# Order changes around seven waits in a two-layer attention, RG-LRU and conv-FFN kernel

## The reference

```python
for l in range(DEPTH):                                   # DEPTH = 2
    mod = (silu(c) @ ada_w[l] + ada_b[l])                # six rows of 1024: shift, scale, gate, twice
    h = rms_norm(x, mix_pre_g[l]) * (1.0 + scale_m) + shift_m
    q, k, v, x_lru, gate = split(h @ w_in[l])            # 512, 128, 128, 512, 512 columns
    attn = sliding_window_attention(rope(q), rope(k), v, sinks[l])
    lru = rg_lru(causal_dwconv(x_lru, 4 taps)) * gelu(gate)
    y = concat([rms_norm(attn, g_attn[l]), rms_norm(lru, g_lru[l])]) @ w_out[l]
    x = x + gate_m * rms_norm(y, mix_post_g[l])
    h = rms_norm(x, ffn_pre_g[l]) * (1.0 + scale_f) + shift_f
    g, val = split(causal_dwconv(h @ ffn_w_up[l], 3 taps))   # 2 x 3072 columns
    y = (gelu(g) * val) @ ffn_w_down[l]
    x = x + gate_f * rms_norm(y, ffn_post_g[l])
```

## Time and profile before

| what | value |
|---|---|
| median of 3 runs | 1156.53 us (1156.14 to 1157.63) |
| profiled execution, its own time | 1151.1 us |
| its span, first to last instruction | 1149.3 us |
| PE busy | 1115.9 us, 97% |
| DVE busy | 803.3 us, 70% |
| ACT busy | 569.6 us, 50% |
| mean granted TensorE clock | 0.991 |

### The profile page before, as it was taken

The page is one execution under the profiler, slowest core; times in us unless marked ns, Lnnn a source line. Parts: engine busy times, 40 slices in busy tenths (PEclk is TensorE's granted clock), DMA queues, the critical chain, the costliest instruction groups (busy, mean ns, idle before and its releaser), DMA issues.

```text
span 1149.3 us, 14253 instructions
## 1 busy us (share of the span) xinstructions
PE 1115.9 (97%) x5638; PEld 936.3 (81%) x5638; DVE 803.3 (70%) x1229; ACT 569.6 (50%) x958; POOL 52.1 (5%) x110
## 2 busy tenths in 40 slices
PE   6999899999999999999998999999999999999997
PEld 6986688888788888888888777898888888888886
DVE  7999987777678776777565797777643665356545
ACT  4488948544134422343377895765422444134431
POOL 3000110000210011000000000000000000000000
PEclk7999999999999999999999999999999999999999
DMA  9853373333765558643132421322232232233221
GB/s 357 337 205 110 100 285 111 128 112 127 270 242 202 167 191 290 158 150 125 55 111 74 93 74 59 102 98 92 96 106 92 92 103 81 91 114 107 92 92 74
DMA packets 49284, 159.88 MB, mean 139 GB/s; under 512 B 9409, under 2 KB 9665, under 8 KB 49217
## 3 DMA queue, kind: packets, MB, share of 16 engines
q1 hardware_dynamic: 33968, 118.57, 30.7%
q0 software_dynamic: 10368, 37.75, 9.9%
q10 hardware_dynamic: 4880, 2.64, 0.9%
HBM read 156.83 MB, written 2.11 MB: 138 GB/s over the span
## 4 chain that ended last, share of the span: by engine, by line
PE 77%; DVE 13%; ACT 5%; DMA 4%; issue 2%; SPq 0%; DVEq 0%; ACTq 0%
PE ps L1832 48%; PE ps L1857 27%; DVE sb_wL L1146 3%; DMA sb_raw<-in_w 1%; ACT sb_wH L604 1%; DMA sb_vw<-in_ada 1%; DMA sb_adaw<-in_ada 1%; DVE sb_x L1224 1%; DVE sb_stage L1152 1%; DVE sb_adaw L1152 1%; PE ps L1945 1%; DVE sb_y L1191 1%; ACT sb_sq L736 1%; DVE sb_xc L1452 1%; DVE sb_vw L1152 0%
## 5 line engine op out<-in xcount | busy, mean ns | idle before, releaser
L1832 PE MATMUL ps<-sb_hH,sb_wH 128*128 128x512 f32 x832 | 325.4, 391 | 0.5 <-ACT sb_xc L807 0.5
L1832 PE MATMUL ps<-sb_hL,sb_wH 128*128 128x512 f32 x832 | 323.8, 389 | 0.0
L1832 PE MATMUL ps<-sb_hH,sb_wL 128*128 128x512 f32 x832 | 323.8, 389 | 0.0
L1146 DVE TENSOR_TENSOR sb_wL<-sb_raw,sb_wH 128x1024 fp32r<-128x1024 f32 x182 | 221.0, 1221 | 78.7 <-ACT sb_wH L604 78.3
L604 ACT ACTIVATE sb_wH<-sb_raw 128x1024 fp32r<-128x1024 f32 x182 | 189.6, 1053 | 163.5 <-DMA sb_raw<-in_w 163.3
L1857 PE MATMUL ps<-sb_wH,sb_mH 128*128 128x512 f32 x512 | 202.2, 395 | 4.6 <-DVE sb_wL L1146 4.6
L1857 PE MATMUL ps<-sb_wL,sb_mH 128*128 128x512 f32 x512 | 199.4, 389 | 0.0
L1857 PE MATMUL ps<-sb_wH,sb_mL 128*128 128x512 f32 x512 | 199.4, 389 | 0.0
L1832 PEld LDWEIGHTS ps<-sb_hH,sb_wH 128*128 128x128 f32 x832 | 156.2, 188 | 37.6 <-issue 4.3
L1832 PEld LDWEIGHTS ps<-sb_hH,sb_wL 128*128 128x128 f32 x832 | 156.2, 188 | 32.5
L1832 PEld LDWEIGHTS ps<-sb_hL,sb_wH 128*128 128x128 f32 x832 | 156.2, 188 | 31.8
(11 more groups left out here) (222 smaller groups left out, 1136.5 us busy)
## 6 DMA issues: line engine op xcount, KB each, us to landing
sb_raw<-in_w SPq DMA_DIRECT2D x182, 512.0 KB, 3.5
sb_adaw<-in_ada POOLq DMA_DIRECT2D x42, 512.0 KB, 4.9
sb_stage<-in_ada SPq DMA_DIRECT2D x24, 512.0 KB, 14.2
sb_vw<-in_ada POOLq DMA_DIRECT2D x20, 512.0 KB, 4.9
sb_raw<-in_w SPq DMA_DIRECT2D x8, 384.0 KB, 14.3
sb_stage<-in_ada POOLq DMA_DIRECT2D x6, 512.0 KB, 4.2
sb_x<-in_x SPq DMA_DIRECT2D x4, 512.0 KB, 5.6
sb_x<-in_xt SPq DMA_DIRECT2D x4, 512.0 KB, 6.6
```

What stands on the lines that cost most here:

```text
L1146: TT(low_of(n), raw_of(n), high_of(n).bitcast(fp32), ALU.subtract).then_inc(w_lo, 1)
L1832: return nc.tensor.matmul(out, a, b, start=start, stop=stop, **kw)
```

## The change

Only the order of calls changes, in the lists of ACT, DVE and PE. No instruction is added, removed or resized, and SP's and POOL's lists stay as they are. The parts:

1. Tile chains, k = 0 and k = 1: ACT and DVE take tile 2 from its second-half square to `x_scaled` ahead of tile 3's square, and tile 2's evictions ahead of (ACT) or behind (DVE) tile 3's norm; the splits of the chunks move. Before, the k = 0 lists had tile 3's square and `y_finish` between.
2. PE, k = 0 only: `transposes(l, 0, 3)` moves from the middle to the end of the second pair.
3. Layer 0 mixer, ACT: `decays(1)` goes behind `gate_tanhs(2)`, `gate_out(1)` goes ahead of a split and of `decays(2)`.
4. Layer 0 mixer, DVE: `attn_low(1)` goes ahead and `drives(1)` behind; `attn_low(2)` goes ahead of `scan(0)` and `drive(1)`; `lo_chunk(O0 + 5)` goes ahead of `product(2)`.
5. Layer 1 mixer, DVE: `lo_chunk(O0 + 5)` goes ahead of `lru_fold(2)` and `product(3)`.
6. Both layers, DVE: `lo_chunk(O0 + 7)` goes ahead of `late(11, 1)`, which is one modulation unit in layer 0 and nothing in layer 1.
7. Down projections, DVE: in each round the low parts go ahead of the units. Layer 1 has no units, so only layer 0 changes.

```diff
@@ tile_chains, ACT
                 split_step(n0 + 2)
+                split_step(n0 + 3)
+                y_square(l, k, 1, 2)
+                y_root(l, k, 2)
                 if k:
-                    split_step(n0 + 3)
-                    y_square(l, k, 1, 2)
-                    y_root(l, k, 2)
-                    x_root(l, k, 2)
-                    x_scaled(l, k, 2)
-                    y_square(l, k, 1, 3)
-                    y_root(l, k, 3)
-                else:
-                    y_square(l, k, 1, 2)
-                    split_step(n0 + 3)
-                    y_root(l, k, 2)
-                    y_square(l, k, 1, 3)
-                    x_root(l, k, 2)
-                    y_root(l, k, 3)
-                    x_scaled(l, k, 2)
+                    split_step(n0 + 4)
+                x_root(l, k, 2)
+                x_scaled(l, k, 2)
+                if k:
+                    split_step(n0 + 5)
+                y_square(l, k, 1, 3)
+                y_root(l, k, 3)
+                tmp_lower(l, k, 2)
                 x_root(l, k, 3)
                 x_scaled(l, k, 3)
-                if k:
-                    split_step(n0 + 4)
-                    split_step(n0 + 5)
-                tmp_lower(l, k, 2)
                 hi_part(l, k, 2, 0)
@@ layer 0 mixer, ACT
                     gate_tanhs(1)
-                    decays(1)
                     square_out(1)
                     attn_high(1)
                     gate_tanhs(2)
+                    decays(1)
+                    gate_out(1)
                     split_step(O0 + 3)
                     decays(2)
-                    gate_out(1)
                     gate_out(2)
@@ tile_chains, DVE
                 lo_part(l, k, 1, 1)
-                if k:
-                    y_finish(l, k, 2)
-                    x_update(l, k, 2)
-                    lo_chunk(n0 + 2)
-                    x_recip(l, k, 2)
-                    lo_chunk(n0 + 3)
-                    y_finish(l, k, 3)
-                else:
-                    lo_chunk(n0 + 2)
-                    y_finish(l, k, 2)
-                    x_update(l, k, 2)
-                    lo_chunk(n0 + 3)
-                    y_finish(l, k, 3)
-                    x_recip(l, k, 2)
+                y_finish(l, k, 2)
+                x_update(l, k, 2)
+                lo_chunk(n0 + 2)
+                x_recip(l, k, 2)
+                lo_chunk(n0 + 3)
+                y_finish(l, k, 3)
                 x_update(l, k, 3)
-                x_recip(l, k, 3)
                 if k:
                     lo_chunk(n0 + 4)
+                x_recip(l, k, 3)
+                tmp_upper(l, k, 2)
+                if k:
                     lo_chunk(n0 + 5)
-                tmp_upper(l, k, 2)
                 lo_part(l, k, 2, 0)
@@ layer 0 mixer, DVE
-                    drives(1)
+                    attn_low(1)
                     gated(1)
                     mod_unit(26)
-                    attn_low(1)
                     gated(2)
+                    drives(1)
                     mod_unit(27)
...
                     drive(0)
+                    attn_low(2)
                     scan(0)
                     drive(1)
-                    attn_low(2)
                     scan(1)
...
                     product(1)
+                    lo_chunk(O0 + 5)
                     product(2)
-                    lo_chunk(O0 + 5)
                     scan(3)
@@ both layers, DVE
                 lo_chunk(O0 + 6)
+                lo_chunk(O0 + 7)
                 late(11, 1)
-                lo_chunk(O0 + 7)
@@ down projections, DVE
                     for r in range(4):
                         fh, pair = divmod(r, 2)
+                        for c in ahead[r]:
+                            lo_chunk(B + down_no(g, 0) + c)
                         units(down_no(g, 2 * r))
                         units(down_no(g, 2 * r + 1))
-                        for c in ahead[r]:
-                            lo_chunk(B + down_no(g, 0) + c)
@@ next_group, PE
-                            if h == 0 and (i, kt) == (1, KT - 1 if k else KT // 2 - 1):
+                            if h == 0 and (i, kt) == (1, KT - 1):
                                 transposes(l, k, 3)
```

## The result

Side by side, four executions each: 1148.95 us (1146.72 to 1149.94) after, 1156.34 us (1156.04 to 1157.63) before, a ratio of 0.9931 [0.9914, 0.9949].

What follows compares the result with a forecast made beforehand. PE was taken as the bound, busy 1115.9 of 1149.3 us, so only its waits count. Terms 5.3 + 1.5 + 1.1 - 1.85 - 1.6 = 4.4 us took the median 1156.5 to 1152.1 us; range 1149.0 to 1155.5.

Steps and rivals of the forecast that it cites:

- the term of layer 1's mixer: Layer 1's mixer: moving `lo_chunk(O0 + 5)` ahead removes PE's 1.07 us wait; gain 1.1 us, bounds 0.8 and 1.1.
- the step that carried the difference between profile and median over unchanged: Whole kernel: the runs' median, 1156.53 us, lies 5.4 us above the profiled execution; this difference was kept for the forecast.
- k = 1: Layer 1's in projection: the 4.10 us wait for `tmp_upper(2)` goes, plus 1.2 us of low clock behind it; gain 5.3 us.
- Up projections: Both layers, k = 0: late transposes leave PE idle about 2.5 us before h = 1; losses 1.85 us and 1.6 us.
- It comes out 0.25 us later: Layer 0's mixer: DVE's modulation unit behind `lo_chunk(O0 + 7)` comes 0.25 us later, counted in layer 0's h = 1 time.
- Layer 0's mixer: Layer 0's mixer: most of some 4 us of waits removed but not gained; term 0, up to 1 us if chain follows PE.
- Down projections: Layer 0's down projections: low parts ahead of units end the 1.43 us wait for D + 6; gain 1.5, bounds 0 and 1.6.
- the units bite back: Rival, layer 0's down projections: evictions of groups 0 and 1 come late, the 1.5 us is lost, 1153.6 us; chance 0.12.
- The clock's rival: Rival, up projections: the clock falls at both new 2.5 us holes; 1154.5 us (chance 0.15) or 1161.1 us (0.06).
- its short form: Up projections: the clock falls at both holes and comes back fast, 1.2 us each: 1154.5 us; chance 0.15.
- its long form: Up projections: the clock stays low for some 10 us of h = 1, 4.5 us per hole: 1161.1 us; chance 0.06.
- all waits simply go: Rival, whole kernel: shown waits of 12.9 us vanish, 1143.6 us; halfway, zero up-projection losses, 1148.6; chance 0.12 for all or half.

Runs made afterwards that it cites:

- tile 3 early: The changed kernel with only PE's edit undone, tile 3's k = 0 transposes back in the middle of the second pair: 1148.64 us, ratio 0.9946 to before.
- the last four runs: Change again 1148.78 us; before with k = 1 lists and O0 + 5 1141.94; before with both zero-matmul fills 1147.97; k = 1, O0 + 5, down projections 1143.10.

## Why the prediction was right, and where it failed

The waits went and came much as forecast. What failed is the term of layer 1's mixer, 1.1 us, together with the step that carried the difference between profile and median over unchanged; the edit measured 5.3 us, and the time came out just below the range.

**k = 1: right in the traces, short in the medians.** The wait is gone by the mechanism given, and the profiled traces show 5.7 for 5.3. What the clock added behind the wait of 4.10 us was seen as well. Alone, the lists gave 10.0 us (5.9 to 12.5 by the interval). The remaining 4.3 I can't settle: in the one execution of that kernel that was profiled the clock did fall in the mixer, but it was the highest of six (1147.16 us, 0.990) and the other five have a higher mean clock. So these lists seem to make that fall rarer; why they should isn't shown.

**Layer 1's mixer: the failed step.** "**gain 1.1 us**, bounds 0.8 and 1.1": the wait is 1.08 us, and the mechanism holds, but in the one usual execution that was traced the wait was followed by some ten microseconds at a granted clock of 0.50, which the term puts at nothing. Alone the edit measured 5.3 us. The step belongs together with "I carry the difference over unchanged": the 5.4 us between the profiled execution and the median were mostly this one fall of the clock (4.8 us in the trace near the median), and the change takes away the wait that sets it off. With 5.3 in place of 1.1 the prediction's own sum is 8.6 us, 1147.9 us, 1.0 below what was measured. That this comes so near is partly luck: the k = 1 lists and this edit together gave 13.7 us and not 5.3 + 5.3, and all parts but k = 0 gave 11.2, so layer 0's other edits added nothing that can be seen. I had looked at the clock only at places where the profile showed it low, and the profile was of an execution in which it wasn't low here.

**Up projections: right in mechanism, too small in layer 0 in the trace.** 2.64 us holes ahead of h = 1, on `hL`, in both layers, as forecast (2.5). Together 3.45 us of loss were forecast; the medians give 4.1 for this part alone and 3.8 to 4.4 by the change without it, which the noise doesn't tell from 3.45. In the two traces layer 1 is as forecast (1.8 for 1.85) and layer 0 is not (2.85 for 1.6). There the step "It comes out 0.25 us later" came out as 1.5, since ACT's splits waited for loads; where the load took as long as in before, it was 0.43. That a transfer could be late there was not in the working.

**Layer 0's mixer: right, as far as the traces go.** The 4 us of waits went and came back as waits of 0.88, 1.23 and 1.41 us at other places; nothing reached the tile chain early. These edits and that at O0 + 7 were in no run by themselves. Not in the prediction is that the clock falls behind the new wait of 1.23 us, in three of the four traces that have it; behind the wait that before has there it falls in three of ten.

**Down projections: not settled in the median.** The two traces give 1.9 us for the term of 1.5, the medians of the run with it and the run without it nothing. No wait on `y_evict` is there. But in one of the five traces with this edit, that with tile 3 early, a unit's load held DVE for 10.39 us and PE for 1.63, so the rival "the units bite back" comes true in some executions. And as the wait itself varies between nothing and 1.7 us, the row of one execution said more than the usual execution has to gain.

**Rivals.** The clock's rival came true in its short form, at 757 (1.4 us, 1.2 forecast), in layer 0 in some executions; its long form, a clock that stays low for some ten microseconds, came true at a place where I had not put it and in before, not in after. So it added to the gain. That all waits simply go was not what happened, though its halfway time, 1148.6, is near the measured one: the 2.64 us holes are there.

**Small slips in the working.** "All others are under 1.7 us" leaves out the waits of 5.4 and 3.3 us at the kernel's start, which stand in both kernels and change nothing. "Low for most of 28 us" was read from one digit of the page: the windows of before show a clock of 0.50 from about 13 to 27 us, half of the slice. The parts named under Chances add up to 0.74 for faster and 0.20 for the same, not 0.76 and 0.18.

## What to carry to other kernels

A single profiled execution that lies well under the median of the runs is a finding, not an offset: look for what the usual execution does that this one doesn't, take another profile until one is near the median, and price each edit in both. Where PE is the bound, a short wait amid light matmuls may cost several times its length by the granted clock behind it (here 1.08 us of wait, 4.8 us behind it in the traced execution). An edit that serves two cases by one list deserves a run for each case: here the k = 1 lists and one moved call give 1141.94 us, and the k = 0 half of the change costs about 4 of the microseconds that the rest brings. And matmuls of zeros in PE's wait, with every dependency left in place, tell what a wait costs by itself from what the clock behind it costs.

## What was not expected of the hardware

After a wait of 1.08 us, behind eight 128x1 matmuls of 0.95 us in all, the granted clock fell to 0.50, the 1.2 GHz level, and stayed there from 706 to 716 us while PE was in work throughout. The same program with a wait of the same length had 1.00 in another execution. Of the 18 executions of before beside the last four runs, three have a mean clock of 0.991 (1149.5 to 1149.6 us), one 0.990 (1152.94) and fourteen 0.984 to 0.988 (1153.5 to 1157.8). Behind waits of 2.64 us amid dense matmuls it fell in some traces and not in others: in the changed kernel it was 0.50 at 757 and 1.00 at 205 in one and the same execution.

```profile
205.00:206.00 1.00, 0.94 (x8) 0.97 (x9) 0.82 (x2) 1.00 (x2) 0.00 (x0) 1.00 0.00 0
```

With only the k = 1 lists it fell in the profiled execution behind the same wait in the mixer, which now stands at 698.5:

```profile
698.00:699.00 1.00, 0.53 (x2) 0.43 (x3) 1.00 (x4) 0.00 (x0) 0.00 (x0) 0.86 0.00 0
699.00:700.00 1.00, 1.00 (x4) 0.81 (x3) 0.45 (x2) 0.00 (x0) 0.00 (x0) 0.50 0.06 16
```

What decides in which execution it falls stays open.
